# Expert loop: a unit's activations are turned in the middle of the next unit's first product

## The reference, cut to what matters

```python
hid = jnp.einsum('nd,edf->nef', xt, exp_w13)     # exp_w13: 16 x 1024 x 512
a, bgl = jnp.split(hid, 2, axis=-1)
act = jax.nn.silu(a) * bgl * gate[:, :, None]
out = jnp.einsum('nef,efd->nd', act, exp_w2)     # exp_w2: 16 x 256 x 1024
```

## Time and profile before

| what | value |
|---|---|
| median of 3 runs | 677.95 us (677.51 to 678.67) |
| profiled execution, its own time | 678.23 us |
| its span | 676.5 us |
| PE busy in the span | 573.5 us (85%) |
| DVE, ACT, POOL busy | 218.8 us, 169.0 us, 50.0 us |
| expert units, first turn to last ACT copy | 440.3 us to 638.8 us |

### The profile page before, as it was taken

The page is one execution under the profiler, slowest core; times in us unless marked ns, Lnnn a source line. Parts: engine busy times, 40 slices in busy tenths (PEclk is TensorE's granted clock), DMA queues, the critical chain, the costliest instruction groups (busy, mean ns, idle before and its releaser), DMA issues.

```text
span 676.5 us, 5896 instructions
## 1 busy us (share of the span) xinstructions
PE 573.5 (85%) x2324; PEld 302.5 (45%) x2324; DVE 218.8 (32%) x390; ACT 169.0 (25%) x293; POOL 50.0 (7%) x67
## 2 busy tenths in 40 slices
PE   2479978999699999999999994289999999999614
PEld 0145534553245555566445554244444444444201
DVE  0333338413912753111143334411212112121067
ACT  0620282647412202333112112000111111011122
POOL 3000000000320210000000000110101001000050
PEclk9789998999899999999999995579999999999957
DMA  9976164048276912400075008536999999972183
GB/s 330 391 216 206 32 194 148 1 135 293 81 267 159 323 34 63 140 0 1 1 300 197 31 31 315 185 95 241 366 341 362 349 347 368 334 267 93 62 326 140
DMA packets 76350, 131.41 MB, mean 194 GB/s; under 512 B 8137, under 2 KB 31010, under 8 KB 76322
## 3 DMA queue, kind: packets, MB, share of 16 engines
q1 hardware_dynamic: 70136, 108.96, 47.1%
q0 software_dynamic: 3744, 13.63, 5.5%
q10 hardware_dynamic: 2442, 8.43, 3.1%
HBM read 112.36 MB, written 18.65 MB: 194 GB/s over the span
## 4 chain that ended last, share of the span: by engine, by line
PE 52%; DVE 8%; ACT 3%; issue 2%; DMA 2%; POOL 1%; POOLq 0%; DVEq 0%; ACTq 0%
PE ms L1188 17%; PE ps L1142 10%; PE ps L1208 9%; PE ps L915 8%; PE ps L1095 1%; PE ms L1127 1%; DVE gd L1685 1%; DMA wring<-expert_rows,yidx 1%; PE ps L1257 1%; PE ps L1085 1%; ACT tmp L865 1%; POOL wring L645 1%; PE ps L1044 1%; DVE tmp L1466 1%; PE ps L1121 1%
## 5 line engine op out<-in xcount | busy, mean ns | idle before, releaser
L915 PE MATMUL ps<-r,wring 128*128 128x512 f32 (+1 forms) x512 | 143.9, 440 | 6.4 <-ACT gd L785 3.9
L915 PEld LDWEIGHTS ps<-r,wring 128*128 128x128 f32 x512 | 79.3, 193 | 70.4 <-issue 68.0
L1142 PE MATMUL ps<-wring,mixT 128*128 128x512 f32 x160 | 69.7, 594 | 0.0
L1188 PE MATMUL ms<-wring,tmp 128*128 128x512 f32 x128 | 56.3, 593 | 1.3 <-DVE tmp L1671 1.3
L1678 DVE SCALAR_TENSOR_TENSOR vtok<-tmp,slot_gate,ms 128x256 f32<-128x256 f32 x16 | 7.7, 481 | 146.5 <-ACT tmp L865 146.5
L1142 PEld LDWEIGHTS ps<-wring,mixT 128*128 128x128 f32 x160 | 30.0, 190 | 36.1 <-issue 36.1
L931 PE MATMUL ps<-wring,cs 128*32 128x512 f32 x192 | 29.0, 754 | 18.7 <-DVE mod L1313 9.4
L618 POOL DMA_INDIRECT mixT<-h_rows,slot_tok x16 | 15.2, 950 | 340.2 <-DVE slot_gate L1664 195.7
L865 ACT ACTIVATE tmp<-ms 128x256 f32<-128x256 f32 x16 | 6.1, 384 | 132.0 <-PE ms L1188 132.0
L1188 PEld LDWEIGHTS ms<-wring,tmp 128*128 128x128 f32 x128 | 24.2, 190 | 31.7 <-issue 30.1
L979 PE MATMUL ps<-wring,r 128*128 128x512 f32 x80 | 35.6, 598 | 1.4 <-ACT vtok L739 1.4
(11 more groups left out here) (266 smaller groups left out, 668.5 us busy)
## 6 DMA issues: line engine op xcount, KB each, us to landing
wring<-in_ada_w_dram SPq DMA_DIRECT2D x12, 2048.0 KB, 11.8
wring<-in_exp_w_dram SPq DMA_DIRECT2D x8, 2048.0 KB, 12.2
r<-in_exp_w_dram SPq DMA_DIRECT2D x4, 2048.0 KB, 11.6
wring<-in_exp_w_dram SPq DMA_DIRECT2D x8, 1024.0 KB, 6.0
tmp<-in_exp_w_dram SPq DMA_DIRECT2D x4, 2048.0 KB, 12.1
expert_rows<-tmp ACTq DMA_DIRECT2D x16, 512.0 KB, 7.5
wring<-in_w_in_dram SPq DMA_DIRECT2D x12, 512.0 KB, 4.3
expert_rows<-zero SPq DMA_DIRECT2D x9, 512.0 KB
```

The costliest lines, as they stand in the source:

```text
L915: i = mm(d, lhsT, r, start=first, stop=last)
L1142: i = mm(dst[:, half * 512:(half + 1) * 512], mixT[:, k, t * P:(t + 1) * P], w[:, k, :], start=(k == 0), stop=(k == KD - 1))
L1188: i = mm(ms[:, b, :], xgT[:, b, k, :], e13[u % 4][:, k, :], start=(k == 0), stop=(k == KD - 1))
```

## The change

`hidden` takes the list of its k steps, and is issued in two halves. Between the halves of unit u+1 stand `turn_a(u)` and `turn_x(u+2)`. On DVE `activate(u+1)` is issued behind `take_a(u)` and `take_x(u+2)`, where `activate(u+2)` stood; `activate(1)` ahead of the loop is gone. No work is added or left out.

```diff
-            def hidden(u):
+            def hidden(u, ks):
                 b = u % 2
                 pe.wait_ge(x_taken, u + 1)
                 pe.wait_ge(e13_in[u % 4], 16 * (u // 4 + 1))
                 if u >= 2:
                     pe.wait_ge(act_ready, u - 1)
-                for k in range(KD):
+                for k in ks:
                     i = mm(ms[:, b, :], xgT[:, b, k, :], e13[u % 4][:, k, :], start=(k == 0), stop=(k == KD - 1))
-                i.then_inc(hid, 1)
+                if k == KD - 1:
+                    i.then_inc(hid, 1)
...
             turn_x(0)
-            hidden(0)
+            hidden(0, range(KD))
             turn_x(1)
-            hidden(1)
             for u in range(NE):
+
+                if u + 1 < NE:
+                    hidden(u + 1, range(0, KD // 2))
                 turn_a(u)
                 if u + 2 < NE:
                     turn_x(u + 2)
+                if u + 1 < NE:
+                    hidden(u + 1, range(KD // 2, KD))
                 output(u)
-                if u + 2 < NE:
-                    hidden(u + 2)
...
             activate(0)
-            activate(1)
             for u in range(NE):
                 take_a(u)
                 if u + 2 < NE:
                     take_x(u + 2)
-                    activate(u + 2)
+                if u + 1 < NE:
+                    activate(u + 1)
```

## The result

The changed kernel takes 668.11 us (median of 4 runs, 667.56 to 669.77) against 678.02 us (4 runs). The medians are 9.9 us or 1.5% apart, where 8.3 us were forecast. The ratio, which is estimated from the runs, is 0.9843, with a 95% interval from 0.9808 to 0.9879; it is not quite the quotient of the two medians, which is 0.9854. Applied to the 677.95 us from which the prediction starts, the ratio gives 667.3 us, under the lower end of the range; the difference of the medians alone would give 668.0 us, just at it.

A forecast was written before the change was run, and what follows sets the result against it. TensorE was taken to bound the expert units, with a wait for DVE's copy. Savings of 6.9 us in 14 units and 1.4 us in unit 14, 8.3 us, gave 669.7 us for the median; range 668.0 to 672.8 us.

The forecast's parts named there:

- The bound and the cause: Expert units: TensorE bounds them, and waits 0.39 us a unit for a copy queued late on DVE.
- The loop's sum: Expert units: 0.49 us less in each of 14 units, 1.4 us in unit 14, 8.3 us in all.
- The added switch and the three added waits: Second half of each first product: taken as costing nothing, at most 0.16 us, 15 times, 2.4 us.
- the router's row: Profile row of transposes followed by matmuls without a pause, 2.58 us; used to price the extra switch at nothing.
- rival A: Turns inside the product: the switch costs 0.16 us × 15 = 2.4 us, giving 672.1 us; chance 0.09.
- The figure of about 62 ns for a matmul: Turns: if weight loads cost this too, ten transposes take 1.24 us and the kernel about 671.8 us.
- The tail: Work behind the expert units: moves earlier as a block, 0 us in the sum.
- the wait of 1.34 us for the sums: DVE behind the units: up to 1.34 us would go if the clock rose sooner; kept for the range only.
- Transfers: Expert units: 4.19 MB a unit asks 368 GB/s at the new pace; deep cover makes the cost nothing.
- ceiling at 354: Expert-unit transfers: if 354 GB/s were the limit, a unit's transfers take 11.85 us; pace set by transfers, 677.4 us, chance 0.04.
- backlog: Weight transfers under that limit: 0.45 us behind in each of 12 units, 5.4 us, leaving 15 us of cover.
- rival C: Expert units: interrupting the product drops the clock to 1.2 GHz, 2.3 us each fall, some 704 us; chance 0.02.

The follow-up runs named there:

- same_again: The changed kernel measured once more with no edit; 670.15 us, ratio 0.9869 to the original kernel.
- turn_after_one: The changed kernel with the turns after the product's first k step instead of the fourth; 669.87 us, ratio 0.9860 to the original kernel.
- The warmed kernels: Kernels with 13 unused matmuls added ahead of the sums: original kernel so edited, ratio 0.9985; changed kernel so edited, 0.9868.
- pe_order_alone: The original kernel with only TensorE's order changed, DVE's order kept; 693.02 us, ratio 1.0213.
- before_again: The original kernel, unchanged, measured against itself; ratio 1.0005, single runs from 676.93 to 679.72 us.
- dve_order_alone: The original kernel with only DVE's order changed, TensorE's order kept; 670.77 us, ratio 0.9895.

## Why the prediction was right or wrong

**The bound and the cause: right.** TensorE's stream bounds the units, and what stood in it was `take_a(u)` queued behind `activate(u+1)`. The two half edits show it: DVE's order alone gives 7.55 of 8.34 us, TensorE's order alone makes the kernel 2.1% slower. The prediction priced the two parts only together; that TensorE's part adds just the 0.8 us of unit 14 is what the experiments add to it.

**The loop's sum: right to 0.1 us.** 11.40 us a unit forecast, 11.39 measured; 8.3 us in all, 8.34 measured, the same in every trace of that loop. DVE's wait for the silu fell from 9.94 to 2.63 us, with 6.19 us of idleness ahead of `take_a`, as it was to. The added switch and the three added waits cost nothing, as the router's row said, so rival A is out: 11.55 us a unit was its sign. The figure of about 62 ns for a matmul (the Trainium skill, "TensorE: Matmul & The Clock Gate", section "Wait — 56ns, not 53.3ns?"), carried over to weight loads, would have given such a unit; the trace does not bear out that carrying over, with ten transposes and their ten loads in 1.09 us, 55 ns each.

**The tail: the step that failed.** The prediction said that "the tail behind the units moves earlier as a block", put 0 us into the sum for it, and kept the wait of 1.34 us for the sums only as a bound. That term was mis-sized: it measured 1.0 us. Behind the loop the two traces of before have 42.00 and 42.16 us, the three of the same loop as the change (the change, same_again, turn_after_one) 40.92, 41.34 and 41.01 us: 1.0 us less on the mean. DVE's waits for the sums account for it: 1.34 and 1.15 us before, none, 0.54 and none with the change. The warmed kernels show that it is the clock at which the sums run. Loop and tail together are 9.3 us, 668.6 us from 677.95, a ratio of 0.986, which is inside the intervals of the change and of same_again. Why the clock rises sooner relative to the sums in the changed kernel is not settled. That they come 8 us earlier is not enough as a reason: in pe_order_alone they come 17 us later than before, and the wait is 0.20 us. With two traces of before against five unwarmed ones of other orders, chance in when it rises isn't ruled out either.

**The range: too narrow below.** Even with the tail's 1.0 us the sum is 668.6 us, inside the range; what put the result under it was spread, and another measurement, same_again, would have put it inside with 669.1. Its lower end, 668.0, had the whole of the 1.34 us but next to nothing for the stages ahead of the loop, which differ by over 2 us between profiles of identical code (454.25 to 456.73 us, once 459.69). In the first 50 us the granted clock was 0.90 in the profile of before and 0.86 in that of the change (first row before, second row changed; each is a line of its own profile):

```profile
0.00:50.00 50.00, 24.67 (x134) 11.05 (x135) 13.45 (x48) 16.85 (x31) 5.28 (x25) 0.90 0.90 316
```
```profile
0.00:50.00 50.00, 24.39 (x136) 11.89 (x137) 13.43 (x48) 16.85 (x31) 5.29 (x25) 0.86 0.91 317
```

The timed runs show the same. Of the 17 runs of before in the group of before_again, the nine with a mean granted clock of 0.932 took 677.36 to 678.46 us, and the three with 0.924 or 0.925 took 679.15 to 681.45 us. By the ratios, the first measurement has 1.3 us more than the 9.3 us of loop and tail, and the second 0.5 us less; by the medians 0.6 us more and 1.3 us less. Both are within such differences, and no run ties the 1.3 us to one stage.

**Transfers: right that they cost nothing, and there was no ceiling at 354.** The mean rose to 369 GB/s with the demand, and no backlog grew: the 2048 KB loads issued from 468 to 582 us landed after 13.2 to 14.6 us. Unit 8's first weights are issued at 502.33 us and used at 535.91 us, 33.6 us later; with 14.1 us to landing 19.5 us are spare, where 15 were reckoned with a backlog. Loads take longer to land (14.3 us against 12.2 us to `wring`), and gathers 7.6 against 5.6 us, all covered. The limit of about 358 GB/s in the Trainium skill ("DMA: Bandwidth & Descriptors", Specifications) did not hold here, where the mean over 91 us is 369 GB/s; the measurement decides.

**The clock: right.** It is 1.00 in the loop; rival C did not occur.

## What to carry to other kernels

On an engine that runs in order, ask of each operation what stands ahead of it in the queue and when that is released: a copy whose input was ready waited here some 0.6 us (it started 1.02 us after the turn, and 0.41 us in the changed kernel) for a silu and an activation of another unit, and changing the order of the two on DVE was worth 7.5 us over the loop. Test the two halves of such a change apart: moving TensorE's work without the other half took away the cover of the wait and lost 15 us, and moving it with the other half gained 0.8. And work on TensorE behind a long idle stretch has a price that depends on when the clock rises: put that spread into the range, or fill the stretch first and compare the rest.

## What was not expected of the hardware

The 16 instructions of the sums behind the units took 9.88 us in before_again and 9.13 us in the profile of the change, after 19.62 and 19.16 us of idleness. In dve_order_alone they took 8.65 us after 19.68 us, so the length of the idleness does not order them; at full clock they take 7.13 us. And the transfers of this loop, at a DMA share of 1.00 before and 1.01 after, carried 352 and then 366 GB/s: a share near 1 did not mean that no more could flow.
